# Causal self-attention of a two-layer decoder trunk: heads by pairs, logits on row halves, values stationary on column halves

## The reference, cut to what matters

```python
logits = jnp.einsum('bqhd,bqjhd->bhqj', qb, kg).astype(jnp.float32) * scale
logits = logits + bias[None, :, None, :]
lse = jax.nn.logsumexp(logits, axis=-1)
p = jnp.exp(logits - lse[..., None]).astype(vg.dtype)
outs.append(jnp.einsum('bhqj,bqjhd->bqhd', p, vg))
...
y = jnp.concatenate([y_attn, y_pool, y_conv], axis=-1)
return y @ w_out
```

## Time and profile before

| | before |
|---|---|
| median of 3 runs | 1365.55 us (1365.31 to 1366.51) |
| profiled execution | 1364.3 us |
| its span in the trace | 1362.5 us |
| TensorE busy, weight loads busy | 98%, 78% of the span |
| VectorE, ScalarE busy | 30%, 24% |
| granted TensorE clock, mean | 0.998 |
| data moved by DMA | 444.59 MB, mean 326 GB/s |

### The profile page before, as it was taken

The page is one execution under the profiler, slowest core; times in us unless marked ns, Lnnn a source line. Parts: engine busy times, 40 slices in busy tenths (PEclk is TensorE's granted clock), DMA queues, the critical chain, the costliest instruction groups (busy, mean ns, idle before and its releaser), DMA issues.

```text
span 1362.5 us, 29767 instructions
## 1 busy us (share of the span) xinstructions
PE 1337.9 (98%) x13261; PEld 1064.5 (78%) x13261; DVE 407.8 (30%) x757; ACT 320.9 (24%) x584; POOL 14.8 (1%) x28
## 2 busy tenths in 40 slices
PE   9999999999999999999999999999999999999986
PEld 7989888888798898898667898557898657898642
DVE  7677555554747753200101100101100101100101
ACT  6445454443644543000000000000000000000001
POOL 1000000000000000000000000000000000000000
PEclk9999999999999999999999999999999999999999
DMA  8925345555553469999999999999999999999994
GB/s 321 325 95 219 124 171 185 185 185 180 187 177 124 156 246 418 419 393 356 411 421 420 419 419 420 421 420 420 420 420 419 421 420 420 418 420 420 421 420 197
DMA packets 63932, 444.59 MB, mean 326 GB/s; under 512 B 7293, under 2 KB 8717, under 8 KB 10936
## 3 DMA queue, kind: packets, MB, share of 16 engines
q1 hardware_dynamic: 61976, 437.22, 80.0%
q0 software_dynamic: 1824, 5.42, 1.1%
HBM read 441.17 MB, written 1.44 MB: 325 GB/s over the span
## 4 chain that ended last, share of the span: by engine, by line
PE 74%; SPq 16%; DMA 4%; DVE 3%; issue 2%; ACT 1%; DVEq 0%; ACTq 0%
PE bank L1923 36%; SPq L451 16%; PE bank L1483 10%; PE bank L1484 10%; PE bank L1485 10%; DMA slot_w_hi<-in_moe_units 2%; DMA slot_w_lo<-in_moe_units 2%; PE bank L1875 2%; PE bank L1989 1%; PE bank L1525 1%; PE bank L1578 1%; DVE w_lo L854 1%; PE bank L1699 1%; PE bank L1619 1%; PE bank L1682 1%
## 5 line engine op out<-in xcount | busy, mean ns | idle before, releaser
L854 DVE TENSOR_TENSOR w_lo<-raw,w_hi 128x1024 fp32r<-128x1024 f32 x154 | 181.2, 1220 | 41.3 <-ACT w_hi L534 40.0
L1410 DVE TENSOR_TENSOR hidden<-hidden,bank 128x384 f32<-128x384 f32 (+1 forms) x56 | 27.3, 488 | 555.0 <-ACT hidden L805 555.0
L534 ACT ACTIVATE w_hi<-raw 128x1024 fp32r<-128x1024 f32 x154 | 154.6, 1055 | 40.0 <-PE bank L1485 39.4
L805 ACT ACTIVATE hidden<-bank 128x384 f32<-128x384 f32 (+1 forms) x56 | 24.5, 438 | 385.8 <-PE bank L1923 385.8
L796 ACT ACTIVATE hT<-bank 128x384 f32<-128x384 f32 (+1 forms) x56 | 24.5, 438 | 297.4 <-PE bank L1989 297.4
L1923 PE MATMUL bank<-raw,mid_x 128*32 128x384 f32 (+1 forms) x1632 | 93.3, 380 | 0.0
L1923 PEld LDWEIGHTS bank<-raw,mid_x 128*32 128x32 f32 x1632 | 89.9, 110 | 2.7 <-issue 2.1
L1483 PE MATMUL bank<-xT_hi,w_hi 128*128 128x256 f32 x320 | 91.8, 287 | 0.0
L1484 PE MATMUL bank<-xT_lo,w_hi 128*128 128x256 f32 x320 | 90.5, 283 | 0.0
L1485 PE MATMUL bank<-xT_hi,w_lo 128*128 128x256 f32 x320 | 90.4, 283 | 0.0
L1483 PE MATMUL bank<-w_hi,xT_hi 128*128 128x512 f32 (+1 forms) x224 | 84.9, 379 | 1.1 <-DVE w_lo L854 0.6
(11 more groups left out here) (339 smaller groups left out, 2087.1 us busy)
## 6 DMA issues: line engine op xcount, KB each, us to landing
raw<-in_moe_units SPq DMA_DIRECT2D x102, 1024.0 KB, 25.8
slot_w_hi<-in_moe_units SPq DMA_DIRECT2D x51, 1024.0 KB, 26.4
slot_w_lo<-in_moe_units SPq DMA_DIRECT2D x50, 1024.0 KB, 26.1
raw<-in_layer_units SPq DMA_DIRECT2D x44, 1024.0 KB, 5.1
raw<-in_dense_units SPq DMA_DIRECT2D x33, 1024.0 KB, 4.9
slot_bias<-in_moe_units SPq DMA_DIRECT2D x17, 1024.0 KB, 26.1
slot_qk<-in_moe_units SPq DMA_DIRECT2D x17, 1024.0 KB, 26.4
slot_xT_lo<-in_moe_units SPq DMA_DIRECT2D x17, 1024.0 KB, 26.7
```

The costliest lines, as they stand in the source:

```text
L534: act.activation(w_hi[:, st.split(u), half, :], raw[:, st.slot(u), half * n:(half + 1) * n], ACT.Copy)\
L805: act.activation(hidden[:, 0:n * P], bank[2][:, 0:n * P], ACT.Silu).then_inc(sem("silu"), 1)
L854: dve.tensor_tensor(w_lo[:, st.split(u), half, :], raw[:, st.slot(u), half * n:(half + 1) * n], w_hi[:, st.split(u), half, :].bitcast(F32) ...
L1410: dve.tensor_tensor(hidden[:, 0:n * P], hidden[:, 0:n * P], bank[j % 2][:, 0:n * P], ALU.mult)\
```

## The change

The heads are worked on in four pairs.

- Logits: the products of the two heads of a pair are issued alternately, the even head on rows 0 to 63 into bank 6, the odd one on rows 64 to 127 into bank 7. The shapes are those of before.
- Probabilities have four buffers instead of two (`probs`; two of them lie where `y_tok` was).
- After the exponentials of a pair VectorE takes the reciprocals of its four sums (`weights`), and ScalarE multiplies the probabilities by them in place (`weigh`, 16 new instructions a layer), before they are transposed. The division after the values, `y_tok` and its eight transposes go.
- Values: the 64 value columns of a head are now the stationary operand, `probT` is moving (256 columns for the first block of keys, 128 for the second). The even head writes partitions 0 to 63, the odd one 64 to 127 of the same bank, so the result comes out as features. Banks 4 and 5 hold two pairs each.
- The pooling products move from bank 6 to bank 5, ahead of the transposes of pair 1, and the values of pair 2 wait until that bank is read. The sums of the output projection exchange the banks 0, 1 and 6, 7.
- The queues of ScalarE and VectorE are rewritten: the split of unit 8 goes ahead of the first exponentials, and the remainders of units 10 and 11 come later than before, between the steps of attention. Units 10 and 11 on TensorE: the first halves stand around the values of the last pair.

```diff
@@ -296,8 +296,8 @@
     eps_col = sb("eps_col", [P, 1])
     ss = sb("ss", [P, NT, 2])
     norm_s = sb("norm_s", [P, 6, NT])
-    mx = sb("mx", [P, 2, NT])
-    nmx = sb("nmx", [P, 2, NT])
+    mx = sb("mx", [P, 4, NT])
+    nmx = sb("nmx", [P, 4, NT])
     den = sb("den", [P, NT, HEADS])
     rden = sb("rden", [P, NT, HEADS])
@@ -358,6 +358,7 @@
     xprobT = [probT[:, h, :].rearrange("p (t m) -> p t m", t=NT) for h in range(2)] + [pool_a[:, :, 16:], pool_b[:, :, 16:]]
     pooled = xn_flat[:, 1024:1536].rearrange("p (b t) -> p b t", b=2)
     y_tok = xn_flat[:, 0:1024].rearrange("p (t f) -> p t f", t=NT)
+    probs = [prob[:, 0, :], prob[:, 1, :], xn_flat[:, 0:512], xn_flat[:, 512:1024]]
     hid = qk_flat[:, 0:1024].rearrange("p (t f) -> p t f", t=NT)
     slots = [raw[:, (MOE_BASE + n) % RAW, :] for n in range(RAW)]
@@ -633,31 +634,57 @@
                        ACT.Copy, scale=DH ** -0.5).then_inc(sem("q_sb"), 1)
     hi(st, 6)
     hi(st, 7)
-    for h in range(HEADS):
...
+    def exps(p):
+        for h in (2 * p, 2 * p + 1):
+            act.wait_ge(sem("logits"), l * HEADS + h + 1)
+            for t, (a, b) in enumerate(((0, P), (P, 3 * P))):
+                act.activation(probs[h % 4][:, a:b], probs[h % 4][:, a:b], ACT.Exp, bias=nmx[:, h % 4, t:t + 1],
+                               accum_out=den[:, t, h:h + 1]).then_inc(sem("exp"), 1)
+    def weigh(p):
+        act.wait_ge(sem("rden"), l * PAIRS + p + 1)
+        for h in (2 * p, 2 * p + 1):
+            for t, (a, b) in enumerate(((0, P), (P, 3 * P))):
+                act.activation(probs[h % 4][:, a:b], probs[h % 4][:, a:b], ACT.Copy, scale=rden[:, t, h:h + 1])\
+                    .then_inc(sem("weighed"), 1)
+    def heads_hi(n):
+        act.wait_ge(sem("pv_mm"), l * PAIRS + 2 * n + 2)
+        act.activation(yT_hi[:, 2 * n:2 * n + 2, :], bank[4 + n][:, :].rearrange("p (k t) -> p k t", k=2), ACT.Copy)\
+            .then_inc(sem("attn_hi"), 1)
+    hi(st, 8)
+    exps(0)
+    hi(st, 9)
+    weigh(0)
+    used(act, st, 7)
+    act.activation(pool_u[:, :, 2:], bank[2][:, :].rearrange("p (b t) -> p b t", b=2), ACT.Copy)\
+        .then_inc(sem("u_sb"), 1)
+    act.activation(conv_c, bank[3][:, :].rearrange("p (b t) -> p b t", b=2), ACT.Copy)\
+        .then_inc(sem("c_sb"), 1)
+    exps(1)
+    hi(st, 10, which=(0,))
+    weigh(1)
+    exps(2)
+    hi(st, 10, which=(1,))
     act.wait_ge(sem("pool_mm"), l1)
     act.wait_ge(sem("params_in"), l * 48 + 64)
     for b in range(2):
-        act.activation(yT_hi[:, 4 + b, :], bank[6][:, b * T:(b + 1) * T], ACT.Copy, scale=pool_s[:, b:b + 1])\
+        act.activation(yT_hi[:, 4 + b, :], bank[5][:, b * T:(b + 1) * T], ACT.Copy, scale=pool_s[:, b:b + 1])\
             .then_inc(sem("pool_hi"), 1)
-    hi(st, 12)
+    hi(st, 11, which=(0,))
+    weigh(2)
+    exps(3)
+    weigh(3)
+    heads_hi(0)
+    hi(st, 11, which=(1,))
+    hi(st, 12, which=(0,))
     act.wait_ge(sem("conv_y"), l1)
     act.activation(yT_hi[:, 6:8, :], conv_y, ACT.Copy).then_inc(sem("conv_hi"), 1)
-    for t in range(NT):
...
+    heads_hi(1)
+    hi(st, 12, which=(1,))
     hi(st, 13, free=(11, 0))
     hi(st, 14, free=(11, 1))
     norm_of_sum(3 * l + 2, 3 * l, (2, 3, 4, 5), st, 15)
@@ -999,54 +1026,71 @@
     def back(buf, k):
         return buf[:, :, 16 - k:16 - k + T]
     if l == 0:
         dve.wait_ge(sem("bias_in"), 16 * (P // SKEW_P))
-    for i in range(HEADS + 1):
...
+    def maxima(p):
+        for h in (2 * p, 2 * p + 1):
             hold(dve, "logits_mm", l * HEADS + h + 1)
-            if h >= 2:
-                hold(dve, "probT_mm", l * HEADS + h - 1)
+            if p >= 2:
+                hold(dve, "probT_mm", l * HEADS + h - 3)
             for t, (a, b, s0) in enumerate(((0, P, P), (P, 3 * P, 0))):
-                c.step(dve.tensor_tensor_reduce(prob[:, h % 2, a:b], bank[6 + h % 2][:, a:b],
+                c.step(dve.tensor_tensor_reduce(probs[h % 4][:, a:b], bank[6 + h % 2][:, a:b],
                                                 bias[:, h, s0:T], 1.0, 3.0 * MASKED, ALU.add, ALU.max,
-                                                mx[:, h % 2, t:t + 1]))
+                                                mx[:, h % 4, t:t + 1]))
             c.wait()
-            dve.tensor_scalar(nmx[:, h % 2, :], mx[:, h % 2, :], -1.0, None, ALU.mult)\
+            dve.tensor_scalar(nmx[:, h % 4, :], mx[:, h % 4, :], -1.0, None, ALU.mult)\
                 .then_inc(sem("logits"), 1)
-        if i >= 1:
-            h = i - 1
+    def weights(p):
+        dve.wait_ge(sem("exp"), l * (2 * HEADS) + 4 * (p + 1))
+        dve.reciprocal(rden[:, :, 2 * p:2 * p + 2], den[:, :, 2 * p:2 * p + 2]).then_inc(sem("rden"), 1)
+    def turned_pair(p):
+        if p:
+            dve.wait_ge(sem("pv_mm"), l * PAIRS + p)
+        for h in (2 * p, 2 * p + 1):
             dve.wait_ge(sem("probT_mm"), l * HEADS + h + 1)
-            if h >= 2:
-                dve.wait_ge(sem("pv_mm"), l * HEADS + h - 1)
             dve.tensor_copy(probT[:, h % 2, 0:3 * P], bank[h % 2][:, 0:3 * P]).then_inc(sem("probT_sb"), 1)
-        if i == 1:
...
+    def heads_lo(n):
+        dve.wait_ge(sem("attn_hi"), l * 2 + n + 1)
+        rest(yT_lo[:, 2 * n:2 * n + 2, :], bank[4 + n][:, :].rearrange("p (k t) -> p k t", k=2),
+             yT_hi[:, 2 * n:2 * n + 2, :]).then_inc(sem("attn_lo"), 1)
+    maxima(0)
+    lo(st, 8, which=(0,))
+    maxima(1)
+    weights(0)
+    lo(st, 8, which=(1,))
+    lo(st, 9)
+    dve.wait_ge(sem("u_sb"), l1)
+    c.link(dve.tensor_tensor(B, U, pool_u[:, :, 1:T + 1], ALU.add))
+    c.step(dve.tensor_tensor(A[64:128, 0, :], B[64:128, 0, :], back(pool_b, 2)[64:128, 0, :], ALU.add))
+    c.link(dve.tensor_tensor(A[:, 1, :], B[:, 1, :], back(pool_b, 2)[:, 1, :], ALU.add))
+    c.link(dve.tensor_tensor(B[:, 1, :], A[:, 1, :], back(pool_a, 4)[:, 1, :], ALU.add))
+    turned_pair(0)
+    weights(1)
+    maxima(2)
+    c.link(dve.tensor_tensor(A[64:128, 1, :], B[64:128, 1, :], back(pool_b, 8)[64:128, 1, :], ALU.add))
+    dve.wait_ge(sem("params_in"), l * 48 + 64)
+    c.step(dve.tensor_tensor(pooled[0:64], B[0:64], pool_inv[0:64, :, :], ALU.mult))
+    c.link(dve.tensor_tensor(pooled[64:128], A[64:128], pool_inv[64:128, :, :], ALU.mult))
+    dve.tensor_tensor(pooled, pooled, U, ALU.subtract).then_inc(sem("pooled"), 1)
+    lo(st, 10, which=(0,))
+    weights(2)
+    turned_pair(1)
+    maxima(3)
+    lo(st, 10, which=(1,))
+    turned_pair(2)
     dve.wait_ge(sem("pool_hi"), l1 * 2)
     for b in range(2):
-        dve.scalar_tensor_tensor(yT_lo[:, 4 + b, :], bank[6][:, b * T:(b + 1) * T], pool_s[:, b:b + 1],
+        dve.scalar_tensor_tensor(yT_lo[:, 4 + b, :], bank[5][:, b * T:(b + 1) * T], pool_s[:, b:b + 1],
                                  yT_hi[:, 4 + b, :].bitcast(F32), ALU.mult, ALU.subtract)\
             .then_inc(sem("pool_lo"), 1)
+    weights(3)
+    lo(st, 11, which=(0,))
     dve.wait_ge(sem("c_sb"), l1)
     used(dve, st, 9)
@@ -1055,14 +1099,7 @@
     for b in range(2):
         c.step(dve.tensor_scalar(conv_y[:, b, :], now_u[:, b, :], conv_w[:, 0, b:b + 1], None, ALU.mult))
     c.wait()
-    dve.wait_ge(sem("exp"), l1 * (2 * HEADS))
...
+    turned_pair(3)
     for tap in (1, 2):
         for b in range(2):
             c.step(dve.scalar_tensor_tensor(conv_y[:, b, :], conv_u[:, b, 2 - tap:2 - tap + T],
@@ -1070,18 +1107,16 @@
         c.wait()
     dve.tensor_tensor(conv_y, conv_y, b_bank[:, :].rearrange("p (b t) -> p b t", b=2), ALU.mult)\
         .then_inc(sem("conv_y"), 1)
-    lo(st, 12, which=(0,))
+    heads_lo(0)
     dve.wait_ge(sem("conv_hi"), l1)
     dve.wait_ge(sem("conv_y"), l1)
     rest(yT_lo[:, 6:8, :], conv_y, yT_hi[:, 6:8, :]).then_inc(sem("conv_lo"), 1)
-    for t in range(NT):
...
+    lo(st, 11, which=(1,))
+    heads_lo(1)
+    lo(st, 12)
     lo(st, 13)
     lo(st, 14)
-    norm_of_sum(3 * l + 2, 7 * l, (0, 1, 6, 7), (2, 3, 4, 5), (12, 13), 15, st)
+    norm_of_sum(3 * l + 2, 7 * l, (6, 7, 0, 1), (2, 3, 4, 5), (12, 13), 15, st)
     for u in range(17, 20):
         lo(st, u)
@@ -1608,64 +1643,80 @@
     pe.wait_ge(sem("q_sb"), l1 * 2)
     pe.wait_ge(sem("k_sb"), l1 * 2)
-    for i in range(HEADS + 2):
...
+    def logits(p):
+        if p:
+            pe.wait_ge(sem("logits"), l * HEADS + 2 * p)
+        for out, queries, keys in ((slice(0, P), slice(0, P), slice(0, P)), (slice(P, 3 * P), slice(P, T), slice(0, T))):
+            for a in range(2):
+                r = slice(a * 64, a * 64 + 64)
+                mm = pe.matmul(bank[6 + a][:, out], qk[r, 0, p, queries], qk[r, 1, p, keys], start=True, stop=True)
+                if out.start:
+                    mm.then_inc(sem("logits_mm"), 1)
+    def turn_pair(p):
+        if p == 0:
+            pe.wait_ge(sem("v_sb"), l1 * 2)
+        else:
+            pe.wait_ge(sem("probT_sb"), l * HEADS + 2 * p)
+        for h in (2 * p, 2 * p + 1):
+            pe.wait_ge(sem("weighed"), l * (2 * HEADS) + 2 * h + 2)
             for b in range(3):
```

(64 more changed lines are left out.)

85 lines of the change are left out of this document (removed).

## The result

The changed kernel takes 1350.55 us (median of 4 runs, 1350.26 to 1350.72), the kernel before 1365.43 us beside it (4 runs, 1365.08 to 1366.51): a ratio of 0.9889 with a 95% interval of 0.9872 to 0.9907. The forecast was 1350.2.

What follows compares the result with a forecast made beforehand. TensorE's queue was taken to bound both attention stages, transfers the expert weights. Terms summed to 36.7 us against 44.57; with 7.7 us saved per layer, 1365.55 - 15.4 = 1350.2 us. Range for 8 in 10: 1348.6 to 1355.5.

Steps and rivals of the forecast that it cites:

- The stage: Each attention stage, 44.57 us before: TensorE's work sums to 36.7 us without waits, 7.7 us saved per layer after small stalls.
- seven projection halves: TensorE in each attention stage: seven halves of 24 projection matmuls, 0.12 us apart, 2.88 us each.
- logits, four pairs: TensorE in each attention stage: a pair of heads costs what one head did, 0.94 us, so 3.8 us.
- values, four pairs: TensorE in each attention stage: both column halves run at once, 0.88 us a pair, against 2 x 0.58 before.
- output halves before the convolution: TensorE late in each attention stage: 24 matmuls ahead of the convolution, 5.5 us, unchanged.
- Row and column halves overlap: TensorE's logits and values: two heads' passes on different row or column halves run at once, 0.94 and 0.88 us a pair.
- The first rivals: Logits or values: row halves don't overlap, 3.0 us a layer back, 4%; column halves don't, 2.6, 4%; neither, 1361.3 us, 1%.
- The rule on weight loads: Values on TensorE: column halves share a row group, exposing four loads a pair, 0.9 us a layer, 1352.0; forecast disagreed.
- The divides: ScalarE in each attention stage: 16 divides of 0.4 to 0.5 us, 5.7 to 7.1 us, bringing it to 27 of 37.
- Slower, by the divides: ScalarE in attention: at 1.5 us a divide nothing is won, at 2 us 1381.8 us; 2%, and 2% for no change.
- VectorE as the bound: VectorE in attention: with work 20% longer the stage stretches 0.7 us, with 30% 2.8; 1351.6 to 1355.8 us; 8%.
- The stream of expert weights: Expert loads follow layer 1's compute, starting at 459 instead of 474 us; rival that only layer 0's gain stays, 1357.9, 2%.

Runs made afterwards that it cites:

- experiment 2: The changed kernel with the two heads' products of each pair parted by a 128x128 transpose: in the logits 1358.55 us, in the values 1357.96 us.

## Why the prediction was right, point by point

**The stage.** Forecast 36.7 us without waits and 36.8 with small stalls, measured 37.01 without any wait. The steps of TensorE's timeline from 52.96 to 89.97 us, added up in the forecast's own terms (an entry of 0.09 counts to the shape that is entered):

| term | forecast | measured |
|---|---|---|
| seven projection halves | 20.2 | 20.57 |
| logits, four pairs | 3.8 | 3.60 |
| values, four pairs | 3.5 | 3.57 |
| transposes of the probabilities | 2.6 | 2.52 |
| pooling products | 1.1 | 1.01 |
| output halves before the convolution | 5.5 | 5.74 |
| sum | 36.7 | 37.01 |

Two terms are over. The first step after another shape is wide: 0.22 us from 53.82 to 54.04 where the later steps are 0.12, and 0.20 to 0.22 at each of the five places where projection work begins again, some 0.4 us together. It was there to be read before the change: of the 3.05 us of a round the forecast took 24 x 0.12 and 0.09 for the entry, and dropped the 0.08 that were left; it had 0.1 for all such steps. And the output halves, "unchanged", lasted 5.58 us before the change (90.22 to 95.80), which the forecast put at 5.5; now they stand in two blocks with the values of the last pair between them, so that their wide step is paid twice:

```profile
83.34 0.47 PE L1518 MATMUL bank<-w_hi,yT_hi 128*128 128x512 f32 x1
83.65 0.39 PE L1519 MATMUL bank<-w_lo,yT_hi 128*128 128x512 f32 x1
...
87.08 0.50 PE L1518 MATMUL bank<-w_hi,yT_hi 128*128 128x512 f32 x1
87.42 0.40 PE L1519 MATMUL bank<-w_lo,yT_hi 128*128 128x512 f32 x1
```

0.31 and 0.34 us where the next steps are 0.23. The logits came out lower because of their four entries only two are in the stage: that of pair 0 lies ahead of its first start, and pair 3 follows the values directly (71.89). The net is 0.2 a layer beyond what was allowed, 0.4 of the 15.4 us. The medians differ by 14.9; what is left is less than the scatter of a median.

That the median was met to 0.35 us is in part luck. The forecast set it 1.25 us above the profiled execution, as before the change. The profiled execution itself, forecast at 1348.9 us, took 1350.7 and was the slowest of the four, 0.15 above their median.

**Row and column halves overlap.** Right: shown by the timeline, and priced by parting them, 4.4 and 4.15 us a stage with the four transposes in it (4 x 0.25). Without them some 3.4 and 3.15 us remain. The first rivals priced the same at 3.0 and 2.6. Both were low for this way of parting, in which each head pays its own first weights and its own exit: 2 x 0.85 against 0.86, and 2 x 0.80 against 0.80.

**The rule on weight loads.** I had weighed the rule of the Trainium skill ("TensorE: Matmul & The Clock Gate", Part 3, "The mechanism") that weight loads overlap matmuls in flight only where the row group differs. By the estimate there it would have cost 0.9 us a layer (16 x 0.05, which is rather 0.8). The traces disagree with it for this shape: the values of a pair, whose two tiles share the rows and differ in columns, take 0.80 us, and those of a single head in experiment 2 take 0.80 as well, so the weights of the second tile cost nothing that shows. Both stream 0.64 us; the 0.16 left agree with the forecast's 0.05 for the first weights and 0.1 for leaving, which no run measures one by one.

**The divides.** Right in size. The groups of the stage after (count | busy us, mean ns | idle before):

```profile
L650 ACT ACTIVATE prob<-prob,rden 128x256 f32<-128x256 f32 x4 | 2.0, 498 | 0.0
...
L650 ACT ACTIVATE prob<-prob,rden 128x128 f32<-128x128 f32 x4 | 1.6, 396 | 1.1 <-DVE rden L1048 1.1
...
L1048 DVE RECIPROCAL rden<-den 128x4 f32<-128x4 f32 x4 | 0.7, 170 | 0.0
```

0.40 and 0.50 us, like the exponentials. ScalarE is busy 24.1 us, not 27. Four divides in a row take 1.50 us from the first start to the last end, so that all 16 add 6.0 and not 7.1; the split of unit 8, two halves and 2.0 us, went ahead of the stage; and the exponentials, four in a row now, overlap in the same way, which may be the 0.6 that is left. The dates, from the first logits, were right to 0.3 us: pair 3 divided by 29.4 (29.6 forecast), pooled features by 19.0 (19.1) for TensorE at 19.8, bank 5 read by 27.7 (27.8), the convolution remainder by 35.3 (35.4).

**Slower, by the divides.** The direction is right, and the break-even near, but by another path than the rival's. It let ScalarE's sum of work fill the stage, at 1.5 us an instruction. By its own steps ScalarE gives a twofold divide 0.70 us (59.60 to 61.00 us for the two of a head) and a threefold one 1.2 (60.88 to 63.26), and the stages are 37.7 and 43.6 us. Drawn on from these two, the stage reaches the old 44.57 at an estimated 1.3 us per divide. ScalarE is busy 36.7 us of the 43.6 there: it doesn't fill the stage, TensorE waits for it at three dates (1.28, 1.75 and 1.29 us). Even threefold, the kernel is still 0.2% faster than before.

**VectorE as the bound.** Right that it was not one (31.2 us of 37.0; the forecast said 31 of 36.8), but undersized as a rival. I priced 20% more work at 0.7 us a stage and 30% at 2.8, by the sum of the work. The sum as it stands (31 x 1.2 = 37.2 against 36.8, and 40.3) gives 0.4 and 3.5, so even these two prices don't follow from it; and the added subtractions, 18%, cost 3.0. What decides is the slack at each date, and that is 0.8 us ahead of the pooling products (19.0 against 19.8) and 1.2 ahead of the values of pair 2. Had VectorE's rows been 20% off, an estimated 1357 us could have been the result, as with the added work, which is outside of my range.

**The stream of expert weights.** Right: loads from 458.8 us (459 forecast), and the two kernels parted in one layer show layer 1 in the total as fully as layer 0. Units 16 and 17, costed at nothing, cost nothing: from the end of the second stage to the first expert loads 27.90 us, before 28.06.

**Last weights.** 1334 forecast, 1335.1 found; the difference is the longer expert stage of this one execution.

## What to carry to other kernels

Two equal products that use different halves of the array's rows, or of its columns, cost the time of one here (0.86 and 0.80 us) if nothing that uses the whole array stands between them in TensorE's queue; put them next to each other and look for the 0.01 us between their starts. What unequal products do, or a narrower instruction between them, was not tried. An operand can be turned so that it fills half the columns even where that alone is slower, if the other half is filled as well. When an engine off the path gets more work, lay out its dates against those of the engine that waits: its busy share over the stage said 84% and promised more room than was there.
